# A decoder trunk's last output chunk: turned tile by tile, with the inverse root applied per token

## The reference

```
o, buf = conv_ffn(h, ffn_prev[i], ffn_w_in[i], ...)      # ends in (silu(a) * v) @ ffn_w_out, 2816 -> 1024
x = x + g2 * rmsnorm(o, norm_ffn_post[i])                # rmsnorm: o * rsqrt(mean(o*o over channels) + eps) * gain
return x
```

## Time and profile before

| | |
|---|---|
| median of 3 runs | 2700.3 us (2697.83 to 2701.5) |
| profiled execution | 2700.66 us, span 2698.9 us |
| mean granted TensorE clock | 0.975 |
| TensorE busy (matmul) | 2575.8 us, 95% |
| VectorE busy | 1229.3 us, 46% |
| ScalarE busy | 814.1 us, 30% |
| GpSimd busy | 135.3 us, 5% |

### The profile page before, as it was taken

How to read it: one execution, slowest core, us unless ns; L and a number is a source line. 1 busy time by engine, 2 the same in 40 slices (tenths; PEclk the granted TensorE clock), 3 DMA queues, 4 the chain that set the end, 5 groups by cost and what they waited for, 6 DMA issues and landing times.

```text
span 2698.9 us, 41295 instructions
## 1 busy us (share of the span) xinstructions
PE 2575.8 (95%) x18190; PEld 2418.6 (90%) x18190; DVE 1229.3 (46%) x1834; ACT 814.1 (30%) x1283; POOL 135.3 (5%) x208
## 2 busy tenths in 40 slices
PE   7999989899999999999999998789899999999997
PEld 5888989899999999999975776569899999999996
DVE  5423237633333334665354445766733333334553
ACT  4211123322222224443333553024422222224442
POOL 1000000000000000000002000200000000000000
PEclk8999999899999999999999999899999999999998
DMA  9576232212212245653210033862222222235653
GB/s 344 206 282 238 70 111 86 91 60 62 61 61 62 63 135 187 199 162 122 67 32 20 23 138 124 330 236 91 84 63 63 63 64 63 63 109 180 195 182 108
DMA packets 323155, 330.78 MB, mean 123 GB/s; under 512 B 14605, under 2 KB 297586, under 8 KB 311133
## 3 DMA queue, kind: packets, MB, share of 16 engines
q1 hardware_dynamic: 301393, 205.48, 24.4%
q0 software_dynamic: 21584, 122.67, 12.0%
HBM read 282.85 MB, written 45.48 MB: 122 GB/s over the span
## 4 chain that ended last, share of the span: by engine, by line
PE 84%; DVE 8%; DMA 3%; ACT 2%; issue 2%; SPq 1%; POOL 0%; DVEq 0%; ACTq 0%; POOLq 0%
PE ps L2059 16%; PE ps L2061 15%; PE ps L2060 15%; PE ps L2109 7%; PE ps L2111 7%; PE ps L2110 7%; PE ps L1934 2%; PE ps L2405 2%; PE ps L2429 2%; PE ps L2378 2%; PE ps L1944 1%; PE ps L2450 1%; PE ps L2332 1%; DVE o_sb L1457 1%; DVE ss_x L1383 1%
## 5 line engine op out<-in xcount | busy, mean ns | idle before, releaser
L2059 PE MATMUL ps<-h_hi,w_hi 128*128 128x344 f32 x2736 | 879.1, 321 | 3.7 <-ACT a_sb L1080 2.1
L2060 PE MATMUL ps<-h_lo,w_hi 128*128 128x344 f32 x2736 | 875.3, 320 | 0.0
L2061 PE MATMUL ps<-h_hi,w_lo 128*128 128x344 f32 x2736 | 875.0, 320 | 0.0
L2059 PEld LDWEIGHTS ps<-h_hi,w_hi 128*128 128x128 f32 x2736 | 516.4, 189 | 9.1 <-issue 4.3
L2061 PEld LDWEIGHTS ps<-h_hi,w_lo 128*128 128x128 f32 x2736 | 516.0, 189 | 0.0
L2060 PEld LDWEIGHTS ps<-h_lo,w_hi 128*128 128x128 f32 x2736 | 515.2, 188 | 0.0
L1304 DVE TENSOR_TENSOR w_lo<-w_raw,w_hi 128x1024 fp32r<-128x1024 f32 (+1 forms) x278 | 325.0, 1177 | 295.3 <-ACT w_hi L888 294.8
L888 ACT ACTIVATE w_hi<-w_raw 128x1024 fp32r<-128x1024 f32 (+1 forms) x278 | 281.5, 1019 | 380.3 <-DMA w_raw<-in_ffn_w_out 145.1
L2109 PE MATMUL ps<-act_hi,w_hi 128*128 128x344 f32 x832 | 268.1, 322 | 7.5 <-ACT sq L959 4.6
L2111 PE MATMUL ps<-act_hi,w_lo 128*128 128x344 f32 x832 | 267.1, 321 | 0.0
L2110 PE MATMUL ps<-act_lo,w_hi 128*128 128x344 f32 x832 | 266.6, 320 | 0.0
(11 more groups left out here) (312 smaller groups left out, 2933.8 us busy)
## 6 DMA issues: line engine op xcount, KB each, us to landing
w_raw<-in_ffn_w_out SPq DMA_DIRECT2D x96, 512.0 KB, 3.5
w_raw<-in_ffn_w_in SPq DMA_DIRECT2D x88, 512.0 KB, 3.7
mod_late<-in_mod_w SPq DMA_DIRECT2D x40, 1024.0 KB, 9.9
w_raw<-in_ffn_w_out SPq DMA_DIRECT2D x48, 384.0 KB, 3.0
act_d<-g_sb POOLq DMA_DIRECT2D x52, 344.0 KB, 3.2
xc<-x_d POOLq DMA_DIRECT2D x12, 1376.0 KB, 6.5
x_d<-xc POOLq DMA_DIRECT2D x9, 1376.0 KB, 5.0
w_raw<-in_sc_w_in SPq DMA_DIRECT2D x24, 512.0 KB, 3.9
```

The source lines that it names most:

```text
L2059: pe.matmul(o, w_hi[k.slot][:, t, :], h_hi[:, t, up_cols(c)], start=t == 0, stop=False)
L2060: pe.matmul(o, w_hi[k.slot][:, t, :], h_lo[:, t, up_cols(c)], start=False, stop=False)
L2061: ins = pe.matmul(o, w_lo[k.slot][:, t, :], h_hi[:, t, up_cols(c)], start=False, stop=t == KD - 1)
```

## The change

For chunk 2 of the last stage alone, the output is made by tokens:

- ScalarE multiplies the prompt columns by the channel gain while it copies a tile to `o_sb`, and copies the sample columns in a second instruction; VectorE multiplies the sample columns by their gains (`sample_gain`).
- TensorE turns each scaled tile and each tile of the old x, by 4 transposes of 128 x 86 into one PSUM bank (`fin_turn`), in the order `FIN`: tiles o0 to o3 after output tile 5, x0 to x7 and o4 to o6 between the blocks of output tile 7, o7 after the channel sums. A turn waits until the bank it writes has been copied out, four items before.
- ScalarE copies each turned item to `y_all` (`fin_out`): items 0 to 3 at the end of its work for tile 6, 4 to 14 before its copy of tile 7, item 15 after the root.
- `spread_o`, `scale_o`, `scale_tiles` and the last four `y_turn` are gone. With 86 tokens on the partitions the inverse root is a column of scalars: four VectorE instructions of 86 x 1024 multiply by it and add x, and after each GpSimd issues a DMA of up to 86 rows; the last one is followed by the DMA of the 8 sample rows.

```diff
+        LAST = 24 * 3 + 2 * KD
+        FIN = [("o", m) for m in range(4)] + [("x", k) for k in range(KD)] + [("o", m) for m in range(4, KD)]
+        def fin_bank(i):
+            return bank([0, 1, 3, 4][i % 4])
+        def last_rows(t, at):
+            return y_all[0:RB, t % 2, :, at + t // 2 * P:at + (t // 2 + 1) * P]
...
 GpSimd:
+            for t in range(4):
+                t0 = (NU - 1) * UC + t * RB
+                n = min(RB, TP - t0)
+                pool.wait_ge(x_new, LAST + t + 1)
+                pool.dma_start(y_prompt[t0:t0 + n, :].rearrange("t (k n) -> t k n", k=KD), last_rows(t, 0)[0:n]
+                               ).then_inc(y_out[t], 16)
+            pool.dma_start(y_sample.rearrange("t (k n) -> t k n", k=KD), last_rows(3, 0)[n:RB]).then_inc(y_out[3], 16)
...
 ScalarE, out_tile:
-                act.activation(o_sb[:, m, :], o, ACT.Copy)
+                if d == 3 and c == 2:
+                    act.activation(o_sb[:, m, 0:PL], o[:, 0:PL], ACT.Copy, scale=mod(1, 5)[:, m, 0:1])
+                    act.activation(o_sb[:, m, PL:UC], o[:, PL:UC], ACT.Copy)
+                else:
+                    act.activation(o_sb[:, m, :], o, ACT.Copy)
...
+            def fin_out(i):
+                what, k = FIN[i]
+                at = 0 if what == "o" else UC
+                act.wait_ge(yt_mm, 12 + i + 1)
+                act.activation(y_all[0:RB, :, k, at:at + 2 * P].rearrange("p z (i n) -> p i z n", i=2),
+                               fin_bank(i)[0:RB, :].rearrange("p (i z n) -> p i z n", i=2, z=2), ACT.Copy).then_inc(yt_ea, 1)
...
+                        if not more and c == 2 and m == 6:
+                            for i in range(4):
+                                act.wait_ge(y_out[i], 16 * (2 if i < 2 else 1))
+                            for i in range(4):
+                                fin_out(i)
+                if not more:
+                    for i in range(4, 15):
+                        fin_out(i)
                 out_tile(d, 2, KD - 1)
                 root(q_post(d, 2))
...
-                    for t0, n in y_tiles(2):
-                        y_out_tile(yt, n)
-                        yt += 1
+                    fin_out(15)
...
 VectorE:
+            def sample_gain(m, G):
+                dve.wait_ge(o_e, LAST + m + 1)
+                dve.tensor_tensor(o_sb[:, m, PL:UC], o_sb[:, m, PL:UC], G[:, m, 1:MLANES], ALU.mult).then_inc(t_done, 1)
...
+                        if m >= 2 and c == 2 and not more:
+                            for k in range(0 if m == 2 else m - 1, m):
+                                sample_gain(k, G)
...
                 inv_root(q_post(d, 2))
-                rs_in(q_post(d, 2))
-                scale_o(d, 2, G)
-                scale_tiles(d, 2, G, range(4))
-                scale_tiles(d, 2, G, range(4, KD))
...
-                    for _, n in y_tiles(2):
-                        y_out_tile(yt, n)
-                        yt += 1
+                    dve.wait_ge(inv_ready, q_post(d, 2))
+                    dve.wait_ge(yt_ea, 6 + len(FIN))
+                    for t in range(4):
+                        dve.scalar_tensor_tensor(last_rows(t, 0), last_rows(t, 0), t_inv[:, t:t + 1], last_rows(t, UC),
+                                                 ALU.mult, ALU.add).then_inc(x_new, 1)
...
 TensorE:
+            def fin_turn(i):
+                what, k = FIN[i]
+                if what == "o":
+                    pe.wait_ge(t_done, LAST + k + 1)
+                else:
+                    pe.wait_ge(xc_in, 16 * NU * 4)
+                pe.wait_ge(yt_ea, 6 + max(0, i - 3))
+                pe.wait_ge(yt_ed, 6)
+                src = (o_sb if what == "o" else xc)[:, k, :]
+                for t in range(4):
+                    ins = trans(fin_bank(i)[0:RB, t * P:(t + 1) * P], src[:, t * RB:(t + 1) * RB])
+                ins.then_inc(yt_mm, 1)
...
+                        if d == 3 and c == 2 and m == KD - 1:
+                            for u, (t, i) in enumerate(zip([1, 3, 5, 7, 9, 11, 13, 15, 17, 18, 20], range(4, 15))):
+                                between[t] = lambda i=i: fin_turn(i)
                         out_tile(d, c, m, between)
+                        if d == 3 and c == 2 and m == 5:
+                            for i in range(4):
+                                fin_turn(i)
...
                     stat_o(q_post(d, 2), d, 2)
-                    spread_o(q_post(d, 2), d, 2)
-                    pe.wait_ge(x_new, 24 * d + KD * NU)
-                    for t, n in y_tiles(2):
-                        y_turn(yt, t, n)
-                        yt += 1
+                    fin_turn(15)
```

More of the change, by code:

```diff
@@ L344, in build @@
     assert off <= A_C
+    y_all = at("y_all", [P, 2, KD, T], A_H)
     y_tok = [at(f"y_tok{i}{z}", [P, KD, T], A_H + z * KD * T4)[:, :, i * P:(i + 1) * P] for i in range(2) for z in range(2)]
@@ L857, in _ @@
             yt = 0
-            for c in range(NU):
+            for c in range(NU - 1):
                 for t0, n in y_tiles(c):
@@ L861, in _ @@
                     pool.wait_ge(yt_ed, yt + 1)
-                    dst = y_sample if t0 == PL and c == NU - 1 else y_prompt[c * UC + t0:c * UC + t0 + n, :]
+                    dst = y_prompt[c * UC + t0:c * UC + t0 + n, :]
                     pool.dma_start(dst.rearrange("t (k n) -> t k n", k=KD), y_tok[yt % 4][0:n]).then_inc(y_out[yt % 4], 16)
@@ L870, in _ @@
                         load_act(3, 5)
+            for t in range(4):
[5 more added lines that the diff above has]
+            pool.dma_start(y_sample.rearrange("t (k n) -> t k n", k=KD), last_rows(3, 0)[n:RB]).then_inc(y_out[3], 16)
             for i in range(4):
-                pool.wait_ge(y_out[i], 16 * ((yt + 3 - i) // 4))
+                pool.wait_ge(y_out[i], 16 * (3, 3, 2, 3)[i])
             pool.wait_ge(tail_out, 16 * 6)
@@ L1596, in down22 @@
                 add_o(d, 2, KD - 1)
+                if not more:
+                    sample_gain(KD - 1, G)
                 inv_root(q_post(d, 2))
-                rs_in(q_post(d, 2))
-                scale_o(d, 2, G)
-                scale_tiles(d, 2, G, range(4))
-                scale_tiles(d, 2, G, range(4, KD))
                 if more:
+                    rs_in(q_post(d, 2))
+                    scale_o(d, 2, G)
+                    scale_tiles(d, 2, G, range(4))
+                    scale_tiles(d, 2, G, range(4, KD))
                     for m in range(1, KD):
```

## The result

The changed kernel takes 2724.05 us (median of 4 runs, 2722.1 to 2729.65) against 2700.9 for the kernel before: ratio 1.0092, 95% interval 1.0072 to 1.0111. It is 23 us slower where 3.9 us less was forecast.

A forecast was written before the change was run, and what follows sets the result against it. It took a full TensorE stream until 2670 us, then a chain with one engine working at a time, as the bound. Terms +7.0 + 0.2 - 10.5 - 0.2 = -3.5 us gave 2697.0 us, 8-in-10 range 2694.4 to 2700.3.

The forecast's parts named there:

- Term 1: Turns moved into TensorE's full stream: 60 transposes and 12 returns to products before its end add 7.0 us.
- Rival (a): The turns in TensorE's stream cost less, 4.7 us, giving a time of 2694.7 us; chance 0.12.
- The cover for ScalarE's late copies: Before item 4's turn, ScalarE has emptied the bank with 1 us to spare; if not, at most 0.6 us lost.
- rival (d): Turns lower TensorE's clock in tile 7; 1.2 GHz for half of it loses 7.9 us, time 2704.9; chance 0.03.
- Term 2: Before the inverse root: the last tile's split copy with a column scale adds 0.2 us.
- Term 3: From inverse root to first output DMA: 2.25 us in place of 12.7, a gain of 10.5 us.
- Term 4: From first output issue to the end: DMA queues stay as full at 265 GB/s, 10.1 us, a gain of 0.2.
- signs by which I wanted to be proved wrong: Stream growth under 5.5 or over 8.5 us, an issue over 1.3 us after its operation, end over 11 after first issue.
- rival (b): The last output issue sets the end as now; a loss of 1.45 us there, time 2698.6; chance 0.13.
- Rival (c): GpSimd's output issues wait for VectorE's four operations, first issue 3.6 us later, time 2701.7; chance 0.05.

The follow-up runs named there:

- b_rows86: The kernel before with only the last chunk's output row counts cut to 86, 86, 86, 78 and 8, no late VectorE scaling: ratio 1.0101.
- v128_sp: v128 with its four last output DMAs issued by SyncE instead of GpSimd: ratio 0.9988 to the kernel before.
- v128: Changed kernel with the last chunk's tokens in three overlapping blocks of 128, shared tokens computed twice and stored once: ratio 0.9982 to the kernel before, then 0.9985.
- a_split80: Changed kernel with each 86-row output DMA replaced by one of 80 and one of 6 rows: ratio 0.9999 to the kernel before.

## Why the prediction was wrong

- Term 1, +7.0 us: right. A gap of four transposes has 0.75 us from product to second next product where 0.314 is usual, 0.44 each, eleven times; items 0 to 3 cost 1.75. Together 6.55. The last product moved by 8.05; the other 1.5 us lie before the first turn, where chunk 2's products begin at 2595.20 instead of 2593.70, mostly in a longer wait for `h_lo` (1.98 us against 0.89). I have not traced that to the change. Rival (a) with 4.7 is out.
- The cover for ScalarE's late copies: right. Item 4's turn came without idle time before it, and TensorE is busy for 84.00 of the 84 us from 2596 to 2680 at granted clock 1.00, 2.4 GHz, so rival (d) did not happen either:

```profile
2596.00:2680.00 84.00, 84.00 (x564) 83.49 (x563) 34.88 (x53) 34.28 (x58) 3.19 (x4) 1.00 0.45 131
```

  The Trainium skill says that the full clock does not engage for transposes (TensorE: Matmul & The Clock Gate, Part 4: PE-mode transpose). This stretch, with 60 of them mixed into the products, shows no loss of clock by them; it does not test transposes alone.
- Term 2, +0.2: measured 3.91 - 3.76 = 0.15. Term 3, from 12.7 to 2.25: measured 2.21, and the four operations had a pitch of (4.87 - 1.28) / 3 = 1.20.
- Term 4 failed: "With the change blocks of 86 tokens come every 1.2 us and take 1.33, so the queues stay just as full." I carried the rate of 265 GB/s over from blocks of 128 and 80 rows, as if bytes alone set it. The first issue to the end took 37.7 us instead of 10.1. These 27.6 us are nearly the whole miss: the span ended at 2724.0 instead of 2695.4, 28.6 us off, and the rest is mostly term 1 (8.05 us at the last product instead of 7.0). What the runs showed in its place: a block of 86 rows goes over two engines, not 16, and takes 20.1 us to land from GpSimd's queue. b_rows86 shows the step by itself: it has none of the change but the row counts. Two of the signs by which I wanted to be proved wrong came true, the end more than 11 us behind the first issue and an issue (the third) over 1.3 us after its operation; the stream's growth of 8.05 us stayed inside its bound of 8.5.
- What I had at hand: the 352 KB block of 88 rows (11 engines by D) took 6.4 us, where the two final 512 KB blocks of 128 rows took 4.4 in the same trace:

```profile
out_y_prompt<-y_tok POOLq DMA_DIRECT2D x2, 512.0 KB, 4.4
```

  I saw the 6.4 in rival (b) and put it down to the x load beside it, at a price of 1.45 us. Two of 16 engines at 265 GB/s for all 16 give an estimate of 10.6 us for the 344 KB of a block instead of 1.33. I cited the Trainium skill (DMA: Bandwidth & Descriptors) for the fixed time of a transfer and not for the number of engines, which by its rule is two for 86 = 2 x 43. Even with the 10.6 us the sum falls short: were the three blocks issued 1.2 us apart and moved side by side, the end would stand at an estimated 1.4 + 2.4 + 10.6 + 2.35 = 16.8 us behind the first issue. The measured 37.7 has blocks of 20.1 us and a third issue 20.5 us after the first.
- Rival (b) priced the wrong thing for the loss, but its mechanism, an end set by the last issue, fits better than term 4's where rows divide well, by the distances of 7.3 to 7.8 us found with v128_sp. v128 gets its 10.0 us because it has four issues, the last at +2.46; five of them, the last at the +4.5 of term 4, would have ended at about +12 by this estimate, as a_split80 does with 12.2. So term 4 had a second, smaller error of some 1.7 us, which the large one covers, and v128's agreement with its 10.1 is luck to that extent.
- Rival (c) did not happen: in the changed kernel the first issue stands at 2686.27, in the middle of VectorE's four operations (2684.09 to 2688.96), and in a_split80 seven issues beside and behind such operations took 4.76 us together.

So the direction of the forecast holds for v128, which is another change, 0.18% faster than before, and not for every good row count: a_split80 keeps the four blocks and comes out at 0.9999.

## What to carry to other kernels

When a change alters the shape of a transfer, count its rows before its bytes: take the largest divisor up to 16, which here was measured for 86 and 85 rows and fits the times at 84, 80 and 128. Then look in the trace at the DMA share, which says roughly how many engines work (one block on two engines gives 2/16 = 0.125 and showed 0.14; two such blocks at once give 0.25 and showed 0.31, small packets included). A tile height chosen for TensorE's or VectorE's convenience (344 = 4 x 86) can be the wrong one for the DMA; overlapping blocks of 128, with the shared rows computed twice and stored once, cost less than such a height. And work put into a saturated TensorE stream is paid in full, so shortening a tail by 10 us this way brought 4 to 5.

## What was not expected of the hardware

- Two rows more or less in a block: 84 rows landed in 7.4 us, 86 in 20.2, 85 in 10.0, 80 in 3.5.
- GpSimd's issue of an 86-row DMA takes 2.6 to 3.2 us instead of 0.86, and with two under way a third came only after 15.3 us of standing still; SyncE's queue too is held, four issues taking 23.65 us. So in these runs slow transfers held the issuing engine, which had nothing else to do.
- Two blocks of 86 rows from GpSimd moved 44 GB/s together (2692 to 2700), one alone from SyncE 43.
- Issuing the output from SyncE started 0.9 us earlier, had its bytes through 1.1 us earlier and ended no earlier.
